# Splitting mixer steps in two, and the gate's copy ahead of the output product, in a two-layer attention and expert kernel

## The chip, the cores and the metric

The kernel runs on one core of a Trainium2 chip. The metric is the device time of one execution in microseconds (us). Three runs of the kernel before gave a median of 4238.35 us, from 4236.18 to 4253.35. A trace of one further execution (4231.16 us, of which 4229.4 lie between its first and last instruction) is what the rows below come from.

## What is computed

Two layers over 5 blocks of 128 tokens (block 0 is the prompt, blocks 1 to 4 the 512 sample tokens), all float32, width 1024. In each layer a block is normalised and modulated, multiplied by one input matrix whose columns feed three parallel mixers, and the mixed heads go through an output product that is gated and added to x. Then a product-key expert layer (PEER) follows: each token picks, for each of 8 heads, 16 of 16384 experts; every expert has one row in `u` and one in `v`.

```
x = x + g1 * (concatenate([o_na, o_pool, o_mla]) @ w_out)          # the output product and its gate
h2 = modulate(rms_norm(x, norm2), sh2, sc2)
x = x + g2 * peer(h2, wq, sub_keys, u, v)

# peer: e = the 16 best experts per head and token, g = softmax of their scores
act = gelu(einsum('nd,nhkd->nhk', xb, u[e]))
y = einsum('nhk,nhkd->nd', g * act, v[e])
```

The input product is cut into A (queries), B (keys), C (values) of the neighbourhood attention, D (pooling input and latent queries) and E (latent keys, rotary keys). A, B, D and E are RMS-normed per head or per row, and so are the up-projected latent queries ("uq") and keys ("ukv").

## The kernel before, in words

Five engines run one list of steps, the plan, each taking from it the steps in which it has work, strictly in the plan's order. The plan is built by `whole_order`.

The expert layer sets the frame. A unit is one head of one block (16 experts), so there are 80 units and 1280 rows. Step `("row", r)` means: GpSimd gathers the v rows for row r - 16 (it waits for TensorE's sum of row r - 20, whose buffer it reuses) and then the u rows for row r + 4 (it waits for VectorE's dot product of row r); VectorE forms the dot product of the u rows with the tokens and does one piece of the search for the best experts of a later unit; ScalarE writes a diagonal matrix of the expert weights; TensorE adds row r - 20 of v into `expert_sum` by two matmuls of 512 columns (the trace records four, and as many weight loads). Both rings have 4 buffers, and one gather moves 512 KB.

`weave` puts the mixer's steps between the rows: every step has a cost (`cost`, an estimate of TensorE's time), and a step is placed after the row at which half of its cost is due. The names that matter here: `pr` (projection A to E of a block), `up` and `kv` (up-projection of queries; assembly of keys), `sc` (scale a projection by its root), `us` and `ks` (the same for up-projected queries and keys, with rotation on GpSimd), `cq`, `tu`, `uT` (transposes on TensorE), `ot` (transposes of the mixed heads), `o` (one half, 512 columns, of the output product), `nx` and `nT` (second norm and its transposes), `q` (queries of the expert layer).

In a step `pr` TensorE multiplies, ScalarE squares the result, VectorE sums the squares of each head (L1432, for A and B) or copies a part (L1464, D; L1469, E), and GpSimd turns the sums into reciprocal roots, `rstd` (L980 and L983). In a step `o` TensorE first writes the gate, spread over 128 partitions, into one PSUM bank (L2052) and then the product into another (L2063). VectorE waits for both, copies the gate to `gated` (L1609), multiplies the product by it (L1611) and adds the result to x (L1614). ScalarE and VectorE count `x_updated` from the last of these. `work` in PSUM has four banks; `Banks.place` gives each result one from the step that fills it to the step that frees it (`fills_of`).

Of the kernel before, what the change touches and what calls it, by code (L numbers as in the profile page):

```python
# [7 lines left out]
D = 1024  # L8
KC = D // P
LAYERS = 2  # L10
NB = 5
# [3 lines left out]
EPS = 1e-6  # L15
HEADS = 6
# [184 lines left out]
def cost(step):  # L201
# [28 lines left out]
def heads_of_prompt(l):  # L230
    b = 0
    return [("pr", "A", l, b), ("pr", "B", l, b), ("sc", "A", l, b), ("pr", "C", l, b), ("tu", "A", l, b),
            ("sc", "B", l, b), ("pr", "D", l, b), ("tu", "B", l, b), ("sc", "D", l, b), ("pr", "E", l, b),
            ("cq", l, b), ("sc", "E", l, b), ("up", l, b), ("ck", l, b), ("us", l, b), ("kp", l, b), ("uT", l, b),
            ("kv", l, b), ("pd", l, 0, 0), ("py", l, 0, b), ("ks", l, b), ("pd", l, 0, 1), ("py", l, 1, b),
            ("kT", l, b)]


def heads_of(l, blocks):
# [6 lines left out]
    for i in range(len(products) + 2):  # L246
        slots += [[("tu", *k) for k in products[i - 2:i - 1] if i >= 2] + [("sc", *k) for k in products[i - 1:i] if i]
                  + [("pr", *k) for k in products[i:i + 1]]]
# [3 lines left out]
    for i in range(n + len(keys) + 2):  # L252
# [6 lines left out]
        out += [("pr", "D", l, b) for b in blocks[i:i + 1]]  # L259
        out += later[j:j + 1] if j >= 0 else []  # L260
        out += [("pr", "E", l, b) for b in blocks[j:j + 1] if j >= 0]
        out += [("up", l, b) for b in blocks[i - 1:i] if i]
# [6 lines left out]
        out += [("kv", l, b) for b in keys[j - 1:j] if j >= 1]  # L269
# [24 lines left out]
def tail(l, t):  # L294
# [102 lines left out]
def fills_of(step):  # L397
# [57 lines left out]
def build(nc, x_prompt, x_sample, c, c_ctx, cache_nat_k, cache_nat_v, cache_mla_ckv, cache_mla_krope,  # L455
# [6 lines left out]
    with ExitStack() as ctx:  # L462
# [172 lines left out]
        for step in plan:  # L635
            kind = step[0]
            if kind == "nx" or kind == "pr" and step[1] != "C":
                stat_turns += [step[1:]]
            elif kind in ("up", "kv"):
                stat_turns += [("uq" if kind == "up" else "ukv", *step[1:])]  # L640
            if kind == "pr" and step[1] != "C" or kind in ("up", "kv"):
                sq_turns += [stat_turns[-1]]
# [86 lines left out]
        pool_in_ready = Steps(sem("pool_in_ready"), [s[2:] if s[0] == "pr" else s[1:] for s in of_kind("pr", "pp")  # L729
                                                             if s[0] == "pp" or s[1] == "D" and not pooled_later(*s[2:])])  # L730
        rope_keys = Steps(sem("rope_keys_copied"), [s[2:] for s in of_kind("pr") if s[1] == "E"])
# [8 lines left out]
        x_updated = Steps(sem("x_updated"), of_kind("o", "fin"))  # L740
# [78 lines left out]
        def _(sp):  # L819
# [46 lines left out]
            def load_gate_bias(l, which):  # L866

                if l:
                    sp.wait_ge(*x_updated.done(("fin", NB - 1) if which else ("o", 0, NB - 1, 1)))
# [90 lines left out]
        def _(pool):  # L960
# [28 lines left out]
            def project(ch, l, b):  # L989
                if ch != "C":  # L990
                    n, mul, add = {"A": (HEADS, 1.0, DH * EPS), "B": (HEADS, 1.0 / DH, EPS),
                                   "D": (1, 1.0 / QR, EPS), "E": (1, 1.0 / KVR, EPS)}[ch]
                    rstd((ch, l, b), n, mul, add)

            def queries_up(l, b):
                rstd(("uq", l, b), HEADS, 1.0, QK * EPS)

            def keys_up(l, b):
                rstd(("ukv", l, b), HEADS, 1.0 / QK, EPS)
# [59 lines left out]
            does = {"nx": norm, "pr": project, "up": queries_up, "kv": keys_up, "us": rope_queries,  # L1059
# [7 lines left out]
        def _(sc):  # L1067
# [11 lines left out]
            def norm(k, l, b):  # L1079
# [3 lines left out]
                if k == "n2":  # L1083
                    sc.wait_ge(*x_updated.done(("o", l, b, 1)))
# [264 lines left out]
        def _(dve):  # L1349
# [107 lines left out]
            def project(ch, l, b):  # L1457

                key = (ch, l, b)
                if ch in "AB":  # L1460
# [747 lines left out]
```

## Time and profile before

| | |
|---|---|
| median of three runs | 4238.35 us |
| profiled execution | 4231.16 us |
| its span | 4229.4 us |
| mean granted TensorE clock | 0.974 |
| TensorE, matmuls | 3607.1 us (85%) |
| VectorE | 2564.7 us (61%) |
| ScalarE | 959.1 us (23%) |
| GpSimd | 2582.1 us (61%) |
| read from HBM | 1511.7 MB |

In the rows below PE is TensorE's matmuls, PEld its weight loads, DVE VectorE, ACT ScalarE, POOL GpSimd and SP SyncE; a trailing q is that engine's sequencer. L with a number is a line of the kernel. An arrow "<-" in a wait names what ended it; "issue" is time in which the engine waited for nothing that the profile shows. Rows of experts begin at 230 us.

### The profile page before, as it was taken

The page shows a single profiled execution, that of the slowest core. Times are in us where ns is not written, and L with a number is a line of the kernel's source. Part 1 is how long each engine was busy: PE and PEld are TensorE (multiplying, and loading weights), DVE is VectorE, ACT ScalarE, POOL GpSimd, SP SyncE. Part 2 cuts the span into 40 slices and gives each one's busy share as a digit, 9 for nine tenths or more (in the row PEclk, how much of TensorE's full clock was granted, in tenths as well). Part 3 has the DMA queues.
Part 4 walks back from the last instruction along what each step waited for, and adds up shares of the span by engine and source line. Part 5 has one row for each costly group of instructions (what it writes and reads, how often), then busy time and mean ns, then how long its engine had stood idle before and what let it go on. Part 6 is the DMA issues. An engine that isn't in the chain of part 4 may idle for free.

```text
span 4229.4 us, 37631 instructions
## 1 busy us (share of the span) xinstructions
PE 3607.1 (85%) x10514; PEld 1679.1 (40%) x10514; DVE 2564.7 (61%) x6453; ACT 959.1 (23%) x2479; POOL 2582.1 (61%) x2833
## 2 busy tenths in 40 slices
PE   7889899989978888888887899999898887777776
PEld 2355444545434223443342355554443432222222
DVE  1175557767655446566666555677676666666664
ACT  1212222223221112222222222232232122221211
POOL 0057446666665556676667663566676677777776
PEclk9899999999999999999999999999999999999999
DMA  6477899999999999999999988999999999999999
GB/s 241 161 266 273 296 337 388 362 389 405 358 367 379 385 390 349 344 356 360 393 401 408 353 290 297 366 367 392 392 407 351 369 402 409 407 405 405 399 403 356
DMA packets 472260, 1519.96 MB, mean 359 GB/s; under 512 B 59980, under 2 KB 78704, under 8 KB 471544
## 3 DMA queue, kind: packets, MB, share of 16 engines
q0 software_dynamic: 368640, 1342.34, 82.2%
q1 hardware_dynamic: 103416, 175.21, 11.6%
q8 instruction: 90, 1.47, 0.1%
q14 instruction: 114, 0.93, 0.1%
HBM read 1511.70 MB, written 5.67 MB: 359 GB/s over the span
## 4 chain that ended last, share of the span: by engine, by line
PE 41%; DMA 27%; POOL 15%; issue 9%; DVE 5%; ACT 2%; SPq 1%; DVEq 0%; POOLq 0%; ACTq 0%
DMA expert_rows<-in_peer_v,experts 22%; PE expert_sum L2112 21%; POOL expert_rows L1033 14%; DMA expert_rows<-in_peer_u,experts 4%; PE work L1871 4%; PE work L1845 3%; PE work L2063 3%; PE work L2078 2%; PE work L2007 2%; PE work L2034 2%; PE work L1819 2%; DVE expert_rows L1779 2%; POOL stat_rstd L983 1%; PE work L2052 1%; PE work L1963 1%
## 5 line engine op out<-in xcount | busy, mean ns | idle before, releaser
L2112 PE MATMUL expert_sum<-expert_rows,weight_diagonals 128*128 128x512 f32 x5080 | 2464.5, 615 | 450.6 <-DMA expert_rows<-in_peer_v,experts 419.8
L1779 DVE CUSTOM_DVE_ANT_0 expert_rows<-expert_rows,tokens 128x1024 f32<-128x1024 f32 x1280 | 1557.0, 1217 | 837.7 <-DMA expert_rows<-in_peer_u,experts 834.0
L1033 POOL DMA_INDIRECT expert_rows<-in_peer_v,experts x1280 | 1231.1, 962 | 915.2 <-PE expert_sum L2112 703.3
L2112 PEld LDWEIGHTS expert_sum<-expert_rows,weight_diagonals 128*128 128x128 f32 x5080 | 904.6, 193 | 1674.7 <-issue 1363.3
L1033 POOL DMA_INDIRECT expert_rows<-in_peer_u,experts x1280 | 1216.6, 950 | 452.8 <-issue 348.5
L1315 ACT ACTIVATE weight_diagonals<-ident,expert_weights 128x128 f32<-128x128 f32 x1270 | 447.2, 392 | 585.5 <-PE expert_sum L2112 355.3
L1871 PE MATMUL work<-weight_ring,h_or_mixed 128*128 128x384 f32 (+3 forms) x800 | 246.6, 462 | 4.1 <-DMA weight_ring<-in_w_in 2.3
L1819 PE MATMUL work<-ident,scratch 128*128 128x128 f32 (+1 forms) x782 | 130.6, 290 | 99.4 <-DVE scratch L1411 36.4
L1845 PE MATMUL work<-weight_ring,silu_cond 128*2 128x512 f32 x384 | 176.1, 613 | 12.0 <-DMA weight_ring<-in_w_mod 11.1
L1871 PEld LDWEIGHTS work<-weight_ring,h_or_mixed 128*128 128x128 f32 x800 | 143.9, 191 | 106.8 <-issue 49.5
L1819 PEld LDWEIGHTS work<-ident,scratch 128*128 128x128 f32 (+1 forms) x782 | 99.4, 146 | 195.3 <-issue 73.5
L1254 ACT ACTIVATE scratch<-work,neg_max 128x640 f32<-128x640 f32 (+3 forms) x120 | 77.3, 644 | 403.8 <-DVE neg_max L1570 403.6
L980 POOL TENSOR_SCALAR stat_biased<-stat_sums 128x6 f32<-128x6 f32 (+1 forms) x82 | 17.6, 214 | 242.8 <-DVE stat_sums L1432 83.8
L2078 PEld LDWEIGHTS work<-h_or_mixed,weight_ring 128*128 128x128 f32 x1024 | 143.9, 196 | 37.3 <-issue 31.4
L2078 PE MATMUL work<-h_or_mixed,weight_ring 128*128 128x128 f32 (+1 forms) x1024 | 153.7, 306 | 5.4 <-DVE h_or_mixed L1423 3.5
L2063 PE MATMUL work<-weight_ring,scratch 128*128 128x512 f32 x320 | 144.2, 604 | 0.0
L1570 DVE TENSOR_REDUCE neg_max<-work 128x1 f32<-128x640 f32 (+3 forms) x120 | 76.3, 635 | 110.7 <-PE work L2007 108.8
L1304 ACT ACTIVATE gelu_dots<-dots 128x16 f32<-128x16 f32 x80 | 17.3, 216 | 442.3 <-DVE dots L1779 441.9
L1779 DVE DVE_READ_ACCUMULATOR2_ANT dots<- 128x1 f32 x1280 | 105.0, 82 | 0.0
L1609 DVE COPY scratch<-work 128x512 f32<-128x512 f32 x20 | 13.8, 692 | 149.8 <-PE work L2063 149.8
L1304 ACT ACT_TABLE_LOAD x78 | 100.1, 1283 | 1.4
L2063 PEld LDWEIGHTS work<-weight_ring,scratch 128*128 128x128 f32 x320 | 59.8, 192 | 83.8 <-issue 83.8
(176 smaller groups left out, 2481.2 us busy)
## 6 DMA issues: line engine op xcount, KB each, us to landing
weight_ring<-in_w_mod SPq DMA_DIRECT2D x24, 2048.0 KB, 11.0
weight_ring<-in_w_out SPq DMA_DIRECT2D x16, 2048.0 KB, 19.4
weight_ring<-in_peer_wq SPq DMA_DIRECT2D x16, 2048.0 KB, 10.0
expert_rows<-in_peer_u,experts POOLq DMA_INDIRECT x1280, 7.3
expert_rows<-in_peer_v,experts POOLq DMA_INDIRECT x1280, 7.3
weight_ring<-in_w_in SPq DMA_DIRECT2D x12, 1536.0 KB, 9.5
weight_ring<-in_w_in SPq DMA_DIRECT2D x4, 2048.0 KB, 15.2
weight_ring<-in_t_pool SPq DMA_DIRECT2D x4, 2048.0 KB, 10.7
```

The lines of the kernel that those rows point to most:

```text
L1033: g.indirect_dma_start(buffer, None, table, bass.IndirectOffsetOnAxis(ap=idx_st[:, col:col + 1], axis=0),).then_inc(row_in, 16)
L1304: a_.activation(gel[:, e * TOPK:(e + 1) * TOPK], dots[:, e * TOPK:(e + 1) * TOPK], ACT.Gelu_apprx_tanh).then_inc(gelu_ready, 1)
L1315: a_.activation(diags[:, at * P:(at + 1) * P], ident[:, :], ACT.Copy, scale=wgt[:, col:col + 1]).then_inc(diag_ready, 1)
L1779: v_.tensor_tensor_reduce(out=u_ring[r % U_RING], in0=u_ring[r % U_RING], in1=tokens[:, :], scale=1.0, scalar=0.0, op0=ALU.mult, op1=ALU.a ...
L1819: ins = t_.transpose(dst[0:n, j * P:(j + 1) * P], v, ident[:, :])
L1845: ins = t_.matmul(dst[0:2, :], sct[:, :].rearrange("p (c k) -> p k c", c=2)[:, kk, :], wt[:, kk, :], start=kk == 0, stop=kk == KC - 1)
L1871: ins = t_.matmul(dst[:, lo:n], hT(b, kk), wt[:, kk, lo:n], start=kk == 0, stop=kk == KC - 1)
L2007: ins = t_.matmul(dst[:, col:col + m * P], lhs, tile(first, m)[lo:lo + n, :, pick, :], start=True, stop=True)
L2034: ins = t_.matmul(dst[:, h * DH:(h + 1) * DH], prob_T[item_no[item] % 2][:, k, :], val, start=k == 0, stop=k == len(blocks) - 1)
L2063: ins = t_.matmul(dst, o_T[:, kk, :], wt[:, kk, :], start=kk == 0, stop=kk == KC - 1)
L2078: ins = t_.matmul(dst[:, 0:len(blocks) * P], wt[:, kk, (h % 4) * P:(h % 4 + 1) * P], h_blocks[:, blocks[0]:blocks[-1] + 1, kk, :], start=k ...
L2112: ins = t_.matmul(acc[:, hf * 512:(hf + 1) * 512], diags[:, at * P:(at + 1) * P], v_buffer(row)[:, hf * 512:(hf + 1) * 512], start=first = ...
```

## The change

Two kinds of step are cut in two. `o` keeps TensorE's part, and a new step `oe` takes VectorE's part (copy, multiplication, addition); each has half of the cost, 4.4. `pr`, `up` and `kv` keep TensorE's and ScalarE's parts, and a new step `hs` of cost 0 takes VectorE's sums or copies and GpSimd's root. Since `weave` places every step by its own cost, a row can now stand between the two parts. In `oe` the wait for the product moves behind the gate's copy.

```diff
-            "kT": 1.3, "py": 0.4, "pp": 3.5, "s": 1.0, "pt": 1.0, "pv": 0.6, "ot": 1.8, "o": 8.8}.get(kind, 0.2)
+            "kT": 1.3, "py": 0.4, "pp": 3.5, "s": 1.0, "pt": 1.0, "pv": 0.6, "ot": 1.8, "o": 4.4, "oe": 4.4,
+            "hs": 0.0}.get(kind, 0.2)
...
-        out += [("pr", "D", l, b) for b in blocks[i:i + 1]]
+        out += [s for b in blocks[i:i + 1] for s in (("pr", "D", l, b), ("hs", "D", l, b))]
...
-        out += [("up", l, b) for b in blocks[i - 1:i] if i]
+        out += [s for b in blocks[i - 1:i] if i for s in (("up", l, b), ("hs", "uq", l, b))]
...
-            out += [("o", l, blocks[i], 0), ("o", l, blocks[i], 1)]
+            out += [s for j in range(2) for s in (("o", l, blocks[i], j), ("oe", l, blocks[i], j))]
...
-        return [(("g", 0, l, b, j), 1, step), (step, 1, step)]
+        return [(("g", 0, l, b, j), 1, ("oe", l, b, j)), (step, 1, ("oe", l, b, j))]
...
+            def head_roots(k, l, b):
+                n, mul, add = {"A": (HEADS, 1.0, DH * EPS), "B": (HEADS, 1.0 / DH, EPS), "D": (1, 1.0 / QR, EPS),
+                               "E": (1, 1.0 / KVR, EPS), "uq": (HEADS, 1.0, QK * EPS),
+                               "ukv": (HEADS, 1.0 / QK, EPS)}[k]
+                rstd((k, l, b), n, mul, add)
...
-            does = {"nx": norm, "pr": project, "up": queries_up, "kv": keys_up, "us": rope_queries,
+            does = {"nx": norm, "hs": head_roots, "us": rope_queries,
                     "ks": rope_keys_of, "row": expert_row}
...
                 dve.wait_ge(*banks.filled(gkey))
-                dve.wait_ge(*banks.filled(step))
                 v_.tensor_copy(gated, bank(gkey)).then_inc(banks.frees(gkey), 1)
                 dve.wait_ge(*banks.freed(gkey))
+                dve.wait_ge(*banks.filled(step))
                 v_.tensor_tensor(gated, bank(step), gated, ALU.mult).then_inc(banks.frees(step), 1)
```

What the orders become is shown at two places. The changed kernel's line numbers differ by 2 to 7. VectorE, layer 0, block 2, first half of the output product (the copy of `work` to `scratch` of 128x512, the multiplication, the addition to x) among dot products ("ISA expert_rows,dots") and pieces of the expert search; before:

```order
1010 L1779 ISA expert_rows,dots<-expert_rows,tokens 128x1024
1011 L1779 ISA dots 128x1
1012 L1676 MAX_INDEX topk<-topk 128x8
1013 L1677 TENSOR_SCALAR topk<-topk 128x1
1014 L1609 COPY scratch<-work 128x512
1015 L1611 TENSOR_TENSOR scratch<-work,scratch 128x512
1016 L1614 TENSOR_TENSOR mla_qkv_or_x_and_queries<-mla_qkv_or_x_and_queries,scratch 128x512
1017 L1779 ISA expert_rows,dots<-expert_rows,tokens 128x1024
```

and of the change, from the dot product on that now follows the same piece of the search:

```order
1015 L1773 ISA dots 128x1
1016 L1675 TENSOR_SCALAR topk<-topk 128x16
1017 L1676 TENSOR_SCALAR topk<-topk 128x16
1018 L1773 ISA expert_rows,dots<-expert_rows,tokens 128x1024
1019 L1773 ISA dots 128x1
1020 L1679 CAST topk<-topk 128x32
1021 L1773 ISA expert_rows,dots<-expert_rows,tokens 128x1024
1022 L1773 ISA dots 128x1
1023 L1683 TENSOR_TENSOR topk<-topk,iota 128x512
1024 L1602 COPY scratch<-work 128x512
1025 L1605 TENSOR_TENSOR scratch<-work,scratch 128x512
1026 L1608 TENSOR_TENSOR mla_qkv_or_x_and_queries<-mla_qkv_or_x_and_queries,scratch 128x512
```

The three instructions moved behind three further expert rows; TensorE's product moved two rows up, so that five rows lie between.

GpSimd, layer 0, from the root of projection D of block 2 (`stat_biased` and `stat_rstd` of 128x1) over that of the up-projected queries of block 1 (128x6) to their rotation (L1014 to L1021); before:

```order
81 L980 TENSOR_SCALAR stat_biased<-stat_sums 128x1
82 L983 TENSOR_TENSOR stat_rstd<-stat_biased,minus_half 128x1
83 L1033 DMA expert_rows<-in_peer_v,experts 128x1024
84 L1033 DMA expert_rows<-in_peer_u,experts 128x1024
85 L1033 DMA expert_rows<-in_peer_v,experts 128x1024
86 L1033 DMA expert_rows<-in_peer_u,experts 128x1024
87 L980 TENSOR_SCALAR stat_biased<-stat_sums 128x6
88 L983 TENSOR_TENSOR stat_rstd<-stat_biased,minus_half 128x6
89 L1033 DMA expert_rows<-in_peer_v,experts 128x1024
90 L1033 DMA expert_rows<-in_peer_u,experts 128x1024
91 L1014 TENSOR_TENSOR scratch<-scratch,bias_or_small_weights 128x6x8 x4
```

and of the change:

```order
81 L1029 DMA expert_rows<-in_peer_v,experts 128x1024
82 L1029 DMA expert_rows<-in_peer_u,experts 128x1024
83 L1029 DMA expert_rows<-in_peer_v,experts 128x1024
84 L1029 DMA expert_rows<-in_peer_u,experts 128x1024
85 L982 TENSOR_SCALAR stat_biased<-stat_sums 128x1
86 L985 TENSOR_TENSOR stat_rstd<-stat_biased,minus_half 128x1
87 L1029 DMA expert_rows<-in_peer_v,experts 128x1024
88 L1029 DMA expert_rows<-in_peer_u,experts 128x1024
89 L982 TENSOR_SCALAR stat_biased<-stat_sums 128x6
90 L985 TENSOR_TENSOR stat_rstd<-stat_biased,minus_half 128x6
91 L1010 TENSOR_TENSOR scratch<-scratch,bias_or_small_weights 128x6x8 x4
```

D's root moved behind the gathers of two rows, the queries' root behind those of one, and between the latter and the rotation no gather is left.

## Rows read from the trace of the kernel before

**Rows 1.** The page's first part, busy time, share and instructions of each engine.

```profile
PE 3607.1 (85%) x10514; PEld 1679.1 (40%) x10514; DVE 2564.7 (61%) x6453; ACT 959.1 (23%) x2479; POOL 2582.1 (61%) x2833
```

**Rows 2.** Waits of VectorE, 230 to 4229 us: us in total, times, longest.

```profile
DVE expert_rows L1779 <- DMA expert_rows<-in_peer_u,experts: 834.0, 778, 7.8
DVE scratch L1609 <- PE work L2063: 132.1, 18, 9.5
...
DVE scratch L1464 <- ACT scratch L1154: 49.3, 7, 8.3
...
DVE stat_sums L1432 <- ACT scratch L1149: 41.6, 10, 6.2
```

**Rows 3.** Waits of GpSimd, 230 to 4229 us.

```profile
POOL expert_rows L1033 <- PE expert_sum L2112: 703.3, 574, 15.7
...
POOL expert_rows L1033 <- DVE dots L1779: 85.3, 167, 3.6
```

**Rows 4.** Order of time, 876 to 900 us: start, length, instruction, [idle before].

```profile
881.00 7.13 PE L2063 MATMUL work<-weight_ring,scratch 128*128 128x512 f32 x16
...
887.97 7.03 PE L2112 MATMUL expert_sum<-expert_rows,weight_diagonals 128*128 128x512 f32 x16
...
888.27 0.69 DVE L1609 COPY scratch<-work 128x512 f32<-128x512 f32 x1 [7.36 <-PE work L2063]
...
889.72 0.69 DVE L1614 TENSOR_TENSOR mla_qkv_or_x_and_queries<-mla_qkv_or_x_and_queries,scratch 128x512 f32<-128x512 f32 x1
...
890.12 1.11 POOL L1033 DMA_INDIRECT expert_rows<-in_peer_v,experts  x1 [6.57 <-PE expert_sum L2112]
...
891.62 1.22 DVE L1779 CUSTOM_DVE_ANT_0 expert_rows<-expert_rows,tokens 128x1024 f32<-128x1024 f32 x1
891.82 0.94 POOL L1033 DMA_INDIRECT expert_rows<-in_peer_u,experts  x1 [0.59 <-DVE dots L1779]
...
895.74 0.69 DVE L1695 TENSOR_TENSOR topk<-topk 128x512 f32<-128x512 f32 x1
895.80 1.44 POOL L1033 DMA_INDIRECT expert_rows<-in_peer_v,experts  x1 [0.30 <-issue]
```

**Rows 5.** Stretches: length, busy PE, PEld, DVE, ACT, POOL, clock, DMA, GB/s.

```profile
888.00:893.00 5.00, 5.00 (x13) 2.25 (x12) 4.66 (x11) 1.78 (x3) 2.06 (x2) 1.00 0.79 273
...
283.00:454.00 171.00, 150.83 (x472) 80.55 (x473) 96.36 (x246) 44.48 (x122) 115.25 (x162) 0.98 0.80 282
...
3600.00:3700.00 100.00, 76.63 (x162) 27.27 (x160) 65.70 (x165) 19.61 (x50) 72.45 (x78) 1.00 1.02 407
```

**Rows 6.** Order of time, 1645 to 1668 us, a projection A of layer 1.

```profile
1655.12 5.31 PE L2112 MATMUL expert_sum<-expert_rows,weight_diagonals 128*128 128x512 f32 x12
...
1656.55 0.21 POOL L980 TENSOR_SCALAR stat_biased<-stat_sums 128x6 f32<-128x6 f32 x1 [1.62 <-DVE stat_sums L1432]
...
1656.84 1.36 POOL L983 TENSOR_TENSOR stat_rstd<-stat_biased,minus_half 128x6 f32<-128x6 f32 x1
...
1658.38 1.04 POOL L1033 DMA_INDIRECT expert_rows<-in_peer_v,experts  x1 [0.19 <-issue]
```

**Rows 7.** Order of time, 302 to 325 us, D and queries of layer 0.

```profile
306.90 0.57 POOL L983 TENSOR_TENSOR stat_rstd<-stat_biased,minus_half 128x1 f32<-128x1 f32 x1
...
307.95 1.01 POOL L1033 DMA_INDIRECT expert_rows<-in_peer_v,experts  x1 [0.47 <-PE expert_sum L2112]
...
313.24 1.35 POOL L983 TENSOR_TENSOR stat_rstd<-stat_biased,minus_half 128x6 f32<-128x6 f32 x1
...
314.91 0.81 DVE L1447 TENSOR_TENSOR scratch<-work,stat_rstd 128x288 f32<-128x288 f32 x2
315.05 0.44 PE L1819 MATMUL work<-ident,scratch 128*128 128x128 f32 x2 [2.01 <-DVE scratch L1491]
...
315.75 0.76 DVE L1455 TENSOR_TENSOR scratch<-scratch,gains 128x576 f32<-128x576 f32 x1
...
317.36 1.48 POOL L1014 TENSOR_TENSOR scratch<-scratch,bias_or_small_weights 128x48 f32<-128x48 f32 x4
```

More of the change, by code:

```diff
@@ L247, in heads_of @@
         slots += [[("tu", *k) for k in products[i - 2:i - 1] if i >= 2] + [("sc", *k) for k in products[i - 1:i] if i]
-                  + [("pr", *k) for k in products[i:i + 1]]]
+                  + [s for k in products[i:i + 1] for s in (("pr", *k), ("hs", *k))]]
     out = [s for slot in slots[:-2] for s in slot] + [("ct", l)] * last
@@ L268, in heads_of @@
         out += [("kT", l, b) for b in keys[j - 2:j - 1] if j >= 2]
-        out += [("kv", l, b) for b in keys[j - 1:j] if j >= 1]
+        out += [s for b in keys[j - 1:j] if j >= 1 for s in (("kv", l, b), ("hs", "ukv", l, b))]
     return out
@@ L636, in build @@
             kind = step[0]
-            if kind == "nx" or kind == "pr" and step[1] != "C":
+            if kind in ("nx", "hs"):
                 stat_turns += [step[1:]]
+            if kind == "pr" and step[1] != "C":
+                sq_turns += [step[1:]]
             elif kind in ("up", "kv"):
-                stat_turns += [("uq" if kind == "up" else "ukv", *step[1:])]
-            if kind == "pr" and step[1] != "C" or kind in ("up", "kv"):
-                sq_turns += [stat_turns[-1]]
+                sq_turns += [("uq" if kind == "up" else "ukv", *step[1:])]
             if kind == "sc":
@@ L728, in build @@
         rope_step = sem("rope_step")
-        pool_in_ready = Steps(sem("pool_in_ready"), [s[2:] if s[0] == "pr" else s[1:] for s in of_kind("pr", "pp")
+        pool_in_ready = Steps(sem("pool_in_ready"), [s[2:] if s[0] == "hs" else s[1:] for s in of_kind("hs", "pp")
                                                              if s[0] == "pp" or s[1] == "D" and not pooled_later(*s[2:])])
-        rope_keys = Steps(sem("rope_keys_copied"), [s[2:] for s in of_kind("pr") if s[1] == "E"])
+        rope_keys = Steps(sem("rope_keys_copied"), [s[2:] for s in of_kind("hs") if s[1] == "E"])
         values_ready = Steps(sem("mla_values_ready"), [s[1:] for s in of_kind("kp")])
@@ L868, in load_gate_bias @@
                 if l:
-                    sp.wait_ge(*x_updated.done(("fin", NB - 1) if which else ("o", 0, NB - 1, 1)))
+                    sp.wait_ge(*x_updated.done(("fin", NB - 1) if which else ("oe", 0, NB - 1, 1)))
                 at = (3 * which + 2) * D
@@ L1083, in norm @@
                 if k == "n2":
-                    sc.wait_ge(*x_updated.done(("o", l, b, 1)))
+                    sc.wait_ge(*x_updated.done(("oe", l, b, 1)))
                     if b == 0:
@@ L1455, in gain_mul, with sums_of_heads @@
                 v_.tensor_tensor(view, view, g, ALU.mult).then_inc(gained.sem, 1)
-            def project(ch, l, b):
-                key = (ch, l, b)
-                if ch in "AB":
+            def sums_of_heads(k, l, b):
+                key = (k, l, b)
+                if k in ("A", "B"):
                     head_sums(key, heads(sq[:, 0:WIDTH]))
-                elif ch == "D" and not pooled_later(l, b):
+                elif k in ("uq", "ukv"):
+                    head_sums(key, heads(sq))
+                elif k == "D" and not pooled_later(l, b):
                     dve.wait_ge(*stats.filled(key))
                     v_.tensor_copy(pool_in[:, max(b - 1, 0), :], bank(key)[:, 0:POOL_W]).then_inc(pool_in_ready.sem, 1)
-                elif ch == "E":
+                elif k == "E":
                     dve.wait_ge(*stats.filled(key))
@@ L1793, in expert_row @@
                     v_.tensor_tensor(block_sum[:, :], acc[:, :], block_sum[:, :], ALU.add).then_inc(sum_copied, 1)
-            does = {"vec": vectors, "mcol": mod_cols, "mrow": gate_row, "nx": norm, "nT": norm_evac, "pr": project, "pp": pool_part, "sc": scale,
-                    "up": queries_up, "us": scale_queries, "kv": assemble, "ks": scale_keys, "py": pooled,
-                    "s": score_maxima, "pt": turn_probs, "pv": head_values, "o": mixer_out, "top": first_topk,
+            does = {"vec": vectors, "mcol": mod_cols, "mrow": gate_row, "nx": norm, "nT": norm_evac, "hs": sums_of_heads, "pp": pool_part, "sc": scale,
+                    "us": scale_queries, "kv": assemble, "ks": scale_keys, "py": pooled,
+                    "s": score_maxima, "pt": turn_probs, "pv": head_values, "oe": mixer_out, "top": first_topk,
                     "fin": finish, "row": expert_row}
```

33 lines of the change are left out of this document (11 added, 22 removed).

## The prediction

> **What bounds the kernel now.** I read the page's busy shares first and then stretches of 100 us and more. TensorE is busy 3607.1 of 4229.4 us, VectorE and GpSimd 61% each [rows 1]. In a stretch that holds expert rows and nothing else the DMA share is 1.02 and the rate 407 GB/s; in the stretch of layer 0's projections, from 283 to 454 us, it is 0.80 and 282 GB/s, with TensorE busy 150.83 of 171 us [rows 5]. So the expert rows, one u and one v row of 512 KB each at a time, want the whole DMA; time is lost only where something keeps GpSimd from issuing the next gather, or where TensorE has so much mixer work that the sums are the pace. The waits of GpSimd say which of the two: between 230 us and the end it waited 703.3 us, 574 times, for an expert sum of TensorE, and 85.3 us, 167 times, for a dot product of VectorE [rows 3].
>
> VectorE's own waits name the steps of this change. It waited 132.1 us, 18 times, for the output product (L2063, in front of the copy L1609); 49.3 us in front of the copy of the pooled part (L1464) and 41.6 us in front of the head sums (L1432), both for ACT squares that stand behind a projection [rows 2]. That is 223 us of a waiting VectorE, but it waited 834.0 us for u rows as well: it has time to spare. Whether these stalls cost anything is decided by what stands behind them, so I then read two products in order of time.
>
> **One output product, read instruction by instruction** [rows 4]. The 16 matmuls of the product take 7.13 us from 881.00. TensorE then sums four rows in 7.03 us from 887.97, so the first sum is there at about 889.7. VectorE starts its copy at 888.27, 7.36 us after it fell idle, adds to x from 889.72, and is free at 890.4. GpSimd had nothing to issue for 6.57 us: the v gather at 890.12 waited for the sum, not for VectorE. Its next gather, of a u row at 891.82, waited 0.59 us for a dot. After that a dot takes VectorE 1.22 us, and GpSimd needs 1.24 us for each gather (0.94 and 0.30 between two) and two gathers per row, so VectorE catches up faster than GpSimd asks. In these 5 us the DMA moved 273 GB/s instead of 407 [rows 5], a loss of 5 x (1 - 273/407) = 1.65 us. The cause of that hole is that TensorE is blocked for 7 us and the v gather in GpSimd's queue stands in front of the u gather. The change leaves both as they are; it takes away only the part that VectorE adds.
>
> **The change part by part.** All sums are against the profiled execution, 4231.16 us (span 4229.4); the median of the runs shown, 4238.35, is 7.2 us above it.
>
> 1. The gate's copy without the wait for the product. Only in three of the 20 places do the two steps stand with no expert row between: both halves of layer 0's prompt, and the first half of its block 1. In the prompt the copy, 0.69 us [rows 4], leaves the chain behind the second product; behind the first the second product hid it in any case. In block 1 it shortens the stall by as much. Sum: -1 us. In the other 17 the copy does not run during the product at all: it now stands 1 to 5 expert rows behind it.
>
> 2. Those 17 steps, VectorE's side. The stall of about 7.3 us goes, since the product is long done when oe comes up. What GpSimd gains is the excess of its waits for dots: 0.59 us where a plain hand-over is 0.30, once or twice per product. 17 x 0.3 = -5 us. From above this is bounded by 0; from below by all excess of the 167 waits, 85.3 - 167 x 0.30 = 35 us [rows 3]. I take -5, since the timeline shows the single event.
>
> 3. The roots (rstd) of projections A and B. Before, GpSimd meets them before the next row's gathers: it waits 1.62 us for the head sums, then works 0.21 + 1.36 us, and its next v gather starts at 1658.38 [rows 6]. Without them the gather could follow the first of the three sums that start at 1655.12 and take 5.31 us, so at about 1657.0: 1.4 us earlier. Nine A and B keys that are followed by sums move so, -13 us. The same 1.57 us come back one to three rows later; where GpSimd waits for a sum then, they are hidden, where it does not, they cost +14. With 703.3 us over 574 waits GpSimd mostly has slack, in these stretches less. Bounds -13 and +1; I take the middle, -6.
>
> 4. The roots of D and E, 15 moved. Before, they lie in a wait: 0.57 us from 306.90, and the v gather at 307.95 then waits another 0.47 us for the sum [rows 7]. Behind a row's gathers they are 0.78 us (0.21 [rows 6] + 0.57) of GpSimd work in the open. Bounds 0 and 15 x 0.78 = +12; I take +3, since GpSimd is idle soon after in most cases.
>
> 5. Scaling of the up-projected queries. In five places (layer 0, blocks 1, 2 and 4; layer 1, blocks 0 and 4) the order now has root, scale and rotation with no expert row between. Before, two gathers lie between the root (from 313.24) and the rotation (317.36), and VectorE's scale and gain (0.81 and 0.76 us) run beside them [rows 7]. Now GpSimd has to wait for them: 0.81 + 0.76 + hand-overs, 1.9 us. Bounds 0 and 5 x 1.9 = +9. Behind the wait stand the gathers of the next row, and VectorE in turn waits for the root (1.35 us) with that row's dot behind it. At 317 us TensorE goes into a 7 us projection, during which GpSimd is idle anyway, so +3.
>
> 6. The scale of D. Its transposes on TensorE waited 2.01 us at 315.05 because VectorE came late, with a row's dot product between head sums and scale [rows 7]. VectorE now has rows done while the projection runs, but its root arrives later. I put it at half, nine D keys x 0.5 = -4; bounds 0 and nine x 2.0 us, of which 9 is the most I believe, since the other waits in this place are shorter.
>
> 7. The addition to x meets other work. A gather that ran beside a VectorE instruction with two SBUF inputs (the 128x512 product of the index search at 895.74) took 1.44 us instead of 0.94 [rows 4]. The addition L1614 has two such inputs. Before it ran where GpSimd had just been released and stretched a gather to 1.11; now it runs in the middle of rows. Bounds 0 and 17 x (0.50 - 0.17) = +6; I take +2.
>
> Here the Trainium skill (SBUF - State Buffer, section Who interferes with whom) speaks against the change: a VectorE instruction with two SBUF inputs contends with a GpSimd instruction that reads SBUF, and the loser is blocked for the whole instruction. The stretched gather agrees. Taken at full length, the page would have each of the 17 additions of 0.69 us hold a gather up by that much, about 12 us as an estimate by that page, where the trace shows 0.50.
>
> TensorE's order: the output products stand up to 3 expert rows earlier than before, each as long as it was. The gate's and the product's banks are held some rows longer. Both at nothing: two of the four banks are left, and the experts' scores need one per 16 rows. If a transpose or a score had to wait for them, each such wait would be a few rows of 2.6 us (1.05 MB at 407 GB/s), and that is in the range, not in the sum.
>
> Sum: -1 - 5 - 6 + 3 + 3 - 4 + 2 = -8, so 4223 us by the profiled execution and 4230 by the median.
>
> **The rivals.**
>
> *The stalls were on the path after all (a real gain).* For it: the chain that ended last does run from the product through copy, product, addition and dots into the gathers; VectorE's stalls add up to 223 us. If each of the 17 holes closed by its 1.65 us, that is -28 in place of the -5, so -31 in all: 4207. With every bound at its lower end (-35, -13, -9, -1) it is -58: 4180. Against it: at 890.12 the gather was released by the sum, and that sum is not earlier.
>
> *GpSimd pays for it (slower).* Roots that lay in waits now stand between gathers. If GpSimd has no slack in the two stretches with projections, items 3, 4, 5 and 7 stand at their upper ends: 1 + 12 + 9 + 6 = +28 with nothing gained: 4266. For it: at 1.24 us per gather two of them take 2.5 us of the 2.6 us that a row takes at full DMA rate, and behind a product GpSimd issues back to back. Against it: TensorE is 88% busy there [rows 5], and GpSimd then waits for it. It decides if GpSimd's waits for sums fall to nearly nothing between 283 and 454 us.
>
> *It doesn't do what it says.* The copy overlaps a product in 3 of 20 places, and if VectorE's stalls were covered in full, the roots in full too, the time stays at 4238.
>
> **How the numbers follow.** My forecast has 0.50, the real gain 0.24, GpSimd pays 0.16, nothing at all 0.10. About 0.5% (21 us, so 4217 and 4260) is what a measurement of this kernel can tell from no change. The gain counts as faster, with 0.02 from the forecast's own low edge: 0.26. Slower is 0.16, and the rest, 0.48 + 0.10 = 0.58, lies within. The range takes in most of each rival: 4190 to 4262. The forecast's own range is 4217 to 4245.
>
> **What would show it.** Right: 17 of the 18 waits in front of the gate's copy gone, and GpSimd's wait for sums behind each output product still 6 to 7 us; the waits for stat_sums in front of the roots near zero, with the lost time under expert_sum in their place; DMA about 273 to 300 GB/s in the 5 us behind a product, as before; a new GpSimd wait of 1 to 2 us in front of the rotation in five places. Wrong: rows between 230 and 631 us, or 1600 and 1900, that advance clearly faster or slower than before, or the hole behind a product gone.

## The result, and the profile after

The changed kernel takes 4265.41 us, median of five runs (4254.86 to 4268.83), against 4238.35 for the kernel before (five runs, 4232.10 to 4253.35). The ratio is 1.0061, 95% interval 1.0046 to 1.0075: the medians are 27 us apart, and the time lies outside the range of 4190 to 4262. The profiled execution took 4256.04 us, its span 4254.2, so 24.8 us more than the span before. The page's first part answers to [rows 1]:

```profile
PE 3625.7 (85%) x10514; PEld 1686.6 (40%) x10514; DVE 2566.1 (60%) x6453; ACT 960.9 (23%) x2479; POOL 2578.0 (61%) x2833
```

No engine has more instructions, and VectorE and GpSimd have the same work to within about 4 us. The time is in waits, and in TensorE's matmuls, as many as before and busy 18.6 us longer (see the granted clock below). VectorE's, from the first expert rows to the end (us in total, times, longest), answer to [rows 2]:

```profile
DVE expert_rows L1773 <- DMA expert_rows<-in_peer_u,experts: 941.0, 819, 8.2
DVE scratch L1443 <- POOL stat_rstd L985: 108.3, 32, 6.4
...
DVE scratch L1489 <- POOL stat_rstd L985: 33.6, 10, 6.6
...
DVE scratch L1462 <- ACT scratch L1150: 19.4, 5, 7.5
...
DVE scratch L1605 <- PE work L2057: 15.6, 4, 6.3
```

The waits that the change was to remove are mostly gone: 132.1 us in front of the copy became 15.6 in front of the multiplication, 49.3 in front of D's copy 19.4. Two other waits took their place. L1443 (head scale, L1447 before) and L1489 (scale of D and E, L1491 before) wait for GpSimd's root. The prediction names this wait in one clause of item 5, for the up-projected queries, and touches it in item 6 for D. In the kernel before, the same two rows read:

```profile
DVE scratch L1447 <- POOL stat_rstd L983: 42.7, 15, 6.1
...
DVE scratch L1491 <- POOL stat_rstd L983: 5.4, 3, 2.1
```

So 48.1 us in 18 waits became 141.9 in 42. GpSimd's waits answer to [rows 3]:

```profile
POOL expert_rows L1029 <- PE expert_sum L2106: 774.4, 614, 14.6
...
POOL scratch L1010 <- DVE scratch L1451: 19.3, 11, 1.8
```

GpSimd waits more for sums, not less: it did not become the bound. It also waits more for dot products, 96.0 us against 85.3. Its waits for head sums (L982) are nearly gone, 8.7 us, as foreseen.

**Where the time is lost.** Every row has one dot product of VectorE, so the time from one dot to a later one compares both kernels stretch by stretch (us, profiled executions; "other chip" is one on which the kernel before takes 4414 us):

| rows | before | after | the change again, other chip | what stands there |
|---|---|---|---|---|
| start to row 0 | 229.8 | 225.4 | 225.7 | prompt |
| 0 to 20 | 52.7 | 61.4 | 61.5 | A and B, layer 0 |
| 20 to 60 | 170.9 | 179.8 | 180.5 | A to E, queries and keys |
| 60 to 400 | 1115.6 | 1115.1 | - | with the output products of layer 0 |
| 400 to 480 | 262.5 | 264.9 | 265.2 | projections of layer 1 |
| 680 to 700 | 86.0 | 96.6 | 95.5 | D and E, layer 1, block 3 |
| 760 to 1279 | 1419.4 | 1416.0 | - | output products, then rows alone |

Three stretches of 80 rows in all lose 8.7 + 8.9 + 10.6 = 28.2 us, and the prompt, 4.4 us shorter for another reason (below), gives 24.8 together with small differences elsewhere. Rows 60 to 400, with the output products of layer 0, neither won nor lost.

**Rows 0 to 20, the first place.** Layer 0, order of time (start, length, instruction, [idle before]); first before, where the dot of 234.45 lies between the head sums and the scale:

```profile
233.99 0.55 DVE L1432 TENSOR_REDUCE stat_sums<-scratch 128x6 f32<-128x384 f32 x1
234.45 1.21 DVE L1779 CUSTOM_DVE_ANT_0 expert_rows<-expert_rows,tokens 128x1024 f32<-128x1024 f32 x1
...
236.56 0.56 DVE L1447 TENSOR_TENSOR scratch<-work,stat_rstd 128x384 f32<-128x384 f32 x1
```

then after, where nothing lies between:

```profile
231.71 0.55 DVE L1428 TENSOR_REDUCE stat_sums<-scratch 128x6 f32<-128x384 f32 x1
...
232.65 1.37 POOL L985 TENSOR_TENSOR stat_rstd<-stat_biased,minus_half 128x6 f32<-128x6 f32 x1
234.16 0.56 DVE L1443 TENSOR_TENSOR scratch<-work,stat_rstd 128x384 f32<-128x384 f32 x1 [1.89 <-POOL stat_rstd L985]
...
236.73 1.05 POOL L1029 DMA_INDIRECT expert_rows<-in_peer_u,experts  x1 [2.71 <-DVE dots L1773]
```

GpSimd needs 1.37 us for the root in either kernel, and 0.20 for a scaling ahead of it [rows 6]. Before, VectorE did a dot and a piece of the search meanwhile; now it stands for 1.89 us, the dot behind it is late, and the next gather, which waits for that dot, is 2.71 us idle. There is no expert sum in these rows, and VectorE waits for hardly anything but roots: VectorE is the pace. Its waits for roots in this stretch, before and after:

```profile
DVE scratch L1447 <- POOL stat_rstd L983: 3.4, 2, 2.0
```

```profile
DVE scratch L1443 <- POOL stat_rstd L985: 11.8, 6, 2.7
```

That is 8.4 us more of waiting in a stretch that is 8.7 us longer.

**Rows 680 to 700, the dearest place.** Projection D of layer 1, block 3, before:

```profile
2451.82 0.42 DVE L1464 COPY scratch<-work 128x256 f32<-128x256 f32 x1 [6.66 <-ACT scratch L1154]
2451.88 0.19 POOL L980 TENSOR_SCALAR stat_biased<-stat_sums 128x1 f32<-128x1 f32 x1 [3.00 <-ACT scratch L1154]
...
2455.16 0.47 DVE L1491 TENSOR_SCALAR scratch<-work,stat_rstd 128x256 f32<-128x256 f32 x1
...
2455.68 0.77 PE L1819 MATMUL work<-ident,scratch 128*128 128x128 f32 x5 [1.06 <-DVE scratch L1491]
```

and after:

```profile
2466.61 0.42 DVE L1462 COPY scratch<-work 128x256 f32<-128x256 f32 x1 [1.89 <-ACT scratch L1150]
...
2467.97 0.94 POOL L1029 DMA_INDIRECT expert_rows<-in_peer_v,experts  x1 [3.81 <-PE expert_sum L2106]
...
2472.99 0.57 POOL L985 TENSOR_TENSOR stat_rstd<-stat_biased,minus_half 128x1 f32<-128x1 f32 x1
2473.67 0.48 DVE L1489 TENSOR_SCALAR scratch<-work,stat_rstd 128x256 f32<-128x256 f32 x1 [6.63 <-POOL stat_rstd L985]
...
2474.20 1.33 PE L1813 MATMUL work<-ident,scratch 128*128 128x128 f32 x5 [4.79 <-DVE scratch L1489]
...
2479.11 1.01 POOL L1029 DMA_INDIRECT expert_rows<-in_peer_v,experts  x1 [5.56 <-PE expert_sum L2106]
```

The long wait in front of D's copy has shrunk from 6.66 to 1.89 us. But the root now stands in GpSimd's queue behind the gathers of two rows, the first of which waits for the sum behind the projection. The root is made 6.4 us after the copy (2472.99 against 2466.61) instead of 0.3. VectorE waits 6.63 us with no row in between, TensorE waits 4.79 us for VectorE with its sums queued behind the transposes, and GpSimd waits for those sums: a circle through three engines. The chain that ended last in this window runs right along it, from the gathers over the root (2472.99) to (start, length, what):

```profile
2473.67 0.49 DVE scratch L1489
...
2474.20 1.33 PE work L1813 x5
2475.53 3.30 PE expert_sum L2106 x4
```

**The granted clock.** In two of the three stretches TensorE also works longer for the same matmuls. Rows 680 to 700 before and after, then rows 20 to 60 after, which answer to the second line of [rows 5] (stretch, length, busy PE, PEld, DVE, ACT, POOL, clock, DMA share, GB/s):

```profile
2441.00:2527.00 86.00, 79.91 (x262) 44.87 (x262) 47.55 (x121) 22.57 (x63) 55.65 (x80) 1.00 0.80 285
```

```profile
2455.00:2552.00 97.00, 84.55 (x266) 47.23 (x265) 48.10 (x122) 23.00 (x63) 56.23 (x81) 0.93 0.74 256
```

```profile
287.00:467.00 180.00, 156.71 (x474) 83.18 (x474) 96.76 (x246) 44.73 (x122) 116.21 (x163) 0.94 0.75 268
```

From 2470 to 2475 us TensorE, waiting for the scale, was busy 0.80 of 5 us; the granted clock was 0.68 in these 5 us and 0.64 in the next five, so in part at the lower of its two levels (1.2 of 2.4 GHz), and 1.00 again from 2480. In the kernel before it was 1.00 in all of rows 680 to 700. Read from the busy times, this makes TensorE about 4 us longer in rows 680 to 700 and about 6 in rows 20 to 60. As an estimate, that is 4 of the 10.6 us and 6 of the 8.9: part of what a root's wait costs is paid behind it, in slower matmuls. No run separates the two. In rows 0 to 20 the clock falls as well (1.00 to 0.92), but VectorE, the pace there, waits for nothing of TensorE's.

**Why the order lost its row.** `hs` has cost 0. `weave` places a step after the row at which half of its cost is due; for a step without cost that is the very end of its product's share. The step that uses the root (`sc`, `us`, `ks`) has cost 0.2, half of which is due at nearly the same point. Before, sums and root stood with the product, at the middle of its share, and one to three rows came before the scale. In 16 places none is left. Call them the uncovered keys: in layer 0 projections A of blocks 1, 2 and 4, B of 2, D of 1, E of 3, the queries of 1, 2 and 4; in layer 1 A of 0 and 4, B and D of 3, E of 4, the queries of 0 and 4. Twelve of them lie in the three stretches that lose time (four, five and three). The other four stand at rows 421, 469, 676 and 678; rows 400 to 480 lose 2.3 us, and rows 480 to 680 nothing (609.5 us before, 608.9 after).

### The profile page after: what moved, and what is told of

Its sections match the earlier page's. It is cut to its first block, busy times and chain, and to the rows that moved or that the text cites. A ratio compares the mean times of both kernels' runs of the same rounds, so it can differ in the third digit from the quotient of the medians.

```text
span 4254.2 us, 37644 instructions
## 1 busy us (share of the span) xinstructions
PE 3625.7 (85%) x10514; PEld 1686.6 (40%) x10514; DVE 2566.1 (60%) x6453; ACT 960.9 (23%) x2479; POOL 2578.0 (61%) x2833
## 4 chain that ended last, share of the span: by engine, by line
PE 41%; DMA 28%; POOL 16%; issue 10%; DVE 4%; ACT 1%; SPq 1%; POOLq 0%; DVEq 0%; ACTq 0%
DMA expert_rows<-in_peer_v,experts 24%; PE expert_sum L2106 23%; POOL expert_rows L1029 14%; PE work L1839 4%; DMA expert_rows<-in_peer_u,experts 3%; PE work L1865 3%; PE work L2057 3%; PE work L2072 2%; PE work L2001 2%; PE work L2028 2%; PE work L1813 2%; POOL stat_rstd L985 1%; DVE expert_rows L1773 1%; PE work L1957 1%; PE work L2046 1%
## 5 line engine op out<-in xcount | busy, mean ns | idle before, releaser
L982 POOL TENSOR_SCALAR stat_biased<-stat_sums 128x6 f32<-128x6 f32 (+1 forms) x82 | 17.6, 214 | 194.8 <-ACT expert_rows L1106 70.9
L1839 PEld LDWEIGHTS work<-weight_ring,silu_cond 128*2 128x2 f32 x384 | 31.3, 86 | 143.8 <-issue 142.1
## 6 DMA issues: line engine op xcount, KB each, us to landing
weight_ring<-in_w_mod SPq DMA_DIRECT2D x24, 2048.0 KB, 10.6
```

The lines of the kernel that those rows point to most:

```text
L1839: ins = t_.matmul(dst[0:2, :], sct[:, :].rearrange("p (c k) -> p k c", c=2)[:, kk, :], wt[:, kk, :], start=kk == 0, stop=kk == KC - 1)
```

## The experiments

All ran on other chips, where the kernel before takes 4413.97 and 4414.92 us (medians of 32 and of 31 runs), so ratios count: 0.1% is 4.4 us there. The times expected for numbers 1 to 4 are those of the first chip, to be read against its 4238 us. Three explanations were on record. COVER: VectorE waits for the roots of the 16 keys because no row covers GpSimd's work. QUEUE: what costs is the root's later place in GpSimd's queue, between gathers. PRODUCT: the halves `oe` cost, by their new place or by the additions beside gathers. In these kernels helper functions stand ahead of `whole_order`, and line numbers are 34 to 41 higher. `rejoin(plan, pick)` puts the picked `hs` or `oe` steps back directly behind their product.

**1. Only the output product split.**

```diff
-    return plan
+    return rejoin(plan, lambda s: s[0] == "hs")
```

> Only the output product is split (o and oe as in the change); every hs stands directly behind its product, as before the change. Theory COVER (the loss is that VectorE now meets 16 scalings with no expert row between the sums and the scaling, and waits for GpSimd's root): none of it is here, 4232 to 4240. Theory QUEUE (31 roots now stand between gathers on GpSimd): the same, 4232 to 4240. Theory PRODUCT (the later addition to x, or the banks held longer, is the loss): 4258 to 4268.

Measured 4411.15 us, ratio 0.9991 (0.9977 to 1.0005). Rows 0 to 20 take 53.4 us, rows 680 to 700 85.7. Its waits:

```profile
DVE scratch L1477 <- POOL stat_rstd L1019: 43.5, 16, 5.8
...
DVE scratch L1639 <- PE work L2091: 16.3, 4, 6.3
```

The product's stall is gone as in the changed kernel, the waits for roots are as before, and the time is the time before. PRODUCT falls. Some 116 us of VectorE's waiting were removed for at most a quarter of a per cent.

**2. Only the sums split**, the output product whole again and at its old place:

```diff
-"o": 4.4, "oe": 4.4,
+"o": 8.8, "oe": 0.0,
...
-    return plan
+    return rejoin(plan, lambda s: s[0] == "oe")
```

> Only the sums and roots are split off (hs as in the change); copy, multiplication and addition stand directly behind the output product, as before, with the copy ahead of the wait. COVER and QUEUE: the whole loss is here, 4260 to 4270. PRODUCT: 4235 to 4245.

Measured 4431.86 us, ratio 1.0040 (1.0023 to 1.0056). The product's stall is there again and still the loss is the change's (1.0048, 1.0033 to 1.0064, for the changed kernel on the same kind of chip, number 5):

```profile
DVE scratch L1477 <- POOL stat_rstd L1019: 107.2, 32, 6.4
DVE scratch L1639 <- PE work L2091: 99.9, 18, 6.7
...
DVE scratch L1523 <- POOL stat_rstd L1019: 32.8, 9, 6.6
```

**3. The row kept.** The change, but the sums of the 16 uncovered keys put back with their products:

```diff
-    return plan
+    return rejoin(plan, lambda s: s[0] == "hs" and uncovered(plan, s))
```

> The change, but the 16 hs steps behind which the use of the root (sc or us) comes with no expert row between, and which had a row before, go back directly behind their product; the other 15 or so stay moved. COVER: the loss goes, the 5 us gained in rows 408 to 460 stay, 4228 to 4240; VectorE's waits for roots fall from 142 us (108.3 + 33.6) to about 60. QUEUE: half of the roots still stand between gathers, 4248 to 4256. PRODUCT: 4260 to 4268.

Measured 4413.56 us, ratio 0.9998 (0.9984 to 1.0012). 16 of the steps `hs` carry the whole loss. VectorE's waits for roots (the two groups above) fell to 78.6 us, not to the expected 60 or so.

**4. The scale later.** The change, its sums and roots where the change has them, but the 16 scalings moved behind the next expert row, so that a row covers the root again:

```diff
+    for step in [s for s in plan if s[0] == "hs" and uncovered(plan, s)]:
+        use = use_of(step)
+        i = plan.index(use)
+        j = next(n for n in range(i, len(plan)) if plan[n][0] == "row")
+        plan = plan[:i] + plan[i + 1:j + 1] + [use] + plan[j + 1:]
```

> The change, but in those 16 places it is the use of the root (sc or us) that moves: behind the next expert row, so that one row lies between the late sums and the scaling again. All roots stand between gathers as in the change. COVER: 4232 to 4246, a little above row_kept, since TensorE's transposes may wait for the later scaling. QUEUE: 4262 to 4270, nothing is mended. PRODUCT: 4262 to 4270.

Measured 4409.57 us, ratio 0.9995 (0.9981 to 1.0010). Number 3 could not tell COVER from QUEUE, since it moves the roots back as well; here they stay late in GpSimd's queue and the loss is gone all the same. But 680 to 700 takes 92.9 us in this kernel's profile, against 87.2 in number 3: there one row does not cover a root that is made 6 us late. In that place the root's later turn between gathers, the term of QUEUE, does count, but by making the wait long.

**5. The changed kernel again**, as the mark for numbers 6 to 8.

> The changed kernel itself, beside the kernel before on this chip, as the measure for the three others: 1.004 to 1.008 times before.

Measured 4436.97 us, ratio 1.0048 (1.0033 to 1.0064). The stretches given in the table above repeat on this chip within 1.1 us.

**6. No wait for the root.** The order of the change on every engine, and GpSimd makes every root in its place, but the 16 scalings multiply by a constant column instead of the root (so their result is another) and need not wait:

```diff
-                r = stat_cols(rst, key, 8)[:, h0:h0 + n]
+                r = (half if key in UNCOVERED else stat_cols(rst, key, 8))[:, h0:h0 + n]
...
-                dve.wait_ge(*rstd_ready.done(key))
+                if key not in UNCOVERED:
+                    dve.wait_ge(*rstd_ready.done(key))
```

> The change with the same instructions in the same order on every engine, but the 16 uncovered scalings take a constant column in place of the root and don't wait for it (their projections come out scaled wrongly); GpSimd makes every root where the change has it. COVER: the loss is this wait, so 0.996 to 1.002 times before. QUEUE (the roots' place between GpSimd's gathers): as the change, 1.004 to 1.008.

Measured 4410.60 us, ratio 0.9994 (0.9980 to 1.0009). At the first place the scale follows the sums at once and the root is made for nobody:

```profile
232.45 0.55 DVE L1466 TENSOR_REDUCE stat_sums<-scratch 128x6 f32<-128x384 f32 x1
232.92 0.55 DVE L1481 TENSOR_TENSOR scratch<-work,minus_half 128x384 f32<-128x384 f32 x1
...
233.38 1.37 POOL L1023 TENSOR_TENSOR stat_rstd<-stat_biased,minus_half 128x6 f32<-128x6 f32 x1
```

Rows 0 to 20 take 53.1 us and rows 680 to 700 85.5, as before. The order of GpSimd's queue is the change's, and by itself it costs nothing that can be measured. QUEUE falls as a cost of its own; this is the run that shows COVER. The granted clock in rows 680 to 700 is 1.00 again, so the slower matmuls go with the wait. From 1.0048 to 0.9994 are 24 us for 16 waits, 1.5 us each on average.

**7. Only the uncovered sums moved**, the other `hs` back with their products:

```diff
-    return plan
+    return rejoin(plan, lambda s: s[0] == "hs" and not uncovered(plan, s))
```

> The opposite of row_kept: of the hs steps only the 16 uncovered ones stand where the change has them, all others go back directly behind their product; the output product is split. COVER: the whole loss, 1.004 to 1.009 times before. QUEUE: half of it, 1.002 to 1.004.

Measured 4440.52 us, ratio 1.0056 (1.0035 to 1.0077): the full loss from the 16 alone, the mirror of number 3. VectorE's waits for roots sum to 106.2 us here, with the whole loss, and to 111.3 us in number 4, with none. So their sum does not tell the cost; in number 4 the wait stands behind the row's dot product instead of in front of it.

**8. More cover than before.** If a covering row is worth 1.5 us, then giving one to places that never had one should make the kernel faster than before. Number 1, with the keys' scalings (`ks`) of eight places that stand right behind their sums moved behind the next row:

```diff
+    plan = rejoin(plan, lambda s: s[0] == "hs")
+    for step in [s for s in plan if s[0] == "hs" and s[1] == "ukv" and rows_between(plan, s, use_of(s)) == 0]:
+        use = use_of(step)
+        i = plan.index(use)
+        rows = [n for n in range(i, len(plan)) if plan[n][0] == "row"]
+        if rows and rows[0] < plan.index(("kT", *use[1:])):
+            plan = plan[:i] + plan[i + 1:rows[0] + 1] + [use] + plan[rows[0] + 1:]
```

> x_only (only the output product is split), and in eight places where the kernel before has sums and scaling of the up-projected keys with no expert row between, the scaling (ks) moves behind the next row. COVER predicts a gain of 8 x about 2 us, 16 us, where TensorE, VectorE and GpSimd set the pace (six of the eight), so 0.996 to 0.998 times before and below both kernels. QUEUE: nothing, 0.998 to 1.001.

Measured 4412.68 us, ratio 1.0003 (0.9987 to 1.0019): a miss, and in the range that was expected of QUEUE. The waits did go:

```profile
DVE scratch L1484 <- POOL stat_rstd L1026: 23.7, 14, 3.8
```

against 43.5 in number 1, and 20 us fewer of waiting bought nothing that can be measured. In the same two profiles VectorE's waits in front of the head sums rose from 84.6 to 99.7 us, so in part it only waited elsewhere. In single profiles rows 20 to 60 take 168.6 us against 171.2 and rows 680 to 700 84.6 against 85.7, but rows 60 to 100 181.2 against 180.0. So 1.5 us is no price of a wait as such. The 16 cost what they do because of where they stand: where VectorE is the pace (rows 0 to 20) or where TensorE has its sums queued behind the scaled result (2474.20 above). This is read from two places in order of time; rows 20 to 60 were not read so, and no run moves single ones of the 16. None of these kernels is measurably faster than the kernel before; the lowest ratio is 0.9991.

## Why the prediction was wrong

The forecast was a sum of -8 us; the change cost 27. By its items:

- **Items 1, 2 and 7, the output product** (-1, -5 and +2, together -4): not contradicted. Number 1 is this part alone, 0.9991 of 4238 or -4 us, but with an interval of -10 to +2, which takes in nothing at all, so the agreement to the microsecond is luck. The reason held. The v gather behind a product still waits for the sum and the DMA's hole is unchanged, against 6.57 us in [rows 4] and 273 GB/s in [rows 5] (the second fence: stretch of 5 us, busy PE, PEld, DVE, ACT, POOL, clock, DMA share, GB/s):

```profile
898.28 0.95 POOL L1029 DMA_INDIRECT expert_rows<-in_peer_v,experts  x1 [6.39 <-PE expert_sum L2106]
899.53 0.94 POOL L1029 DMA_INDIRECT expert_rows<-in_peer_u,experts  x1 [0.30 <-issue]
```

```profile
896.00:901.00 5.00, 5.00 (x13) 2.24 (x12) 2.68 (x7) 0.80 (x2) 2.11 (x3) 1.00 0.80 263
```

  The 0.59 us in front of the u gather became 0.30, just the bit that item 2 counted. Item 7's +2 was not there: 7 of the 20 additions held a gather up in the profile after, by 0.09 to 0.48 us and 2.0 us in all, against 17 and 2.9 us before. The sign that it named came only in part: 14 of the 18 waits went, not 17. Four remain, now in front of the multiplication.
- **Items 3 and 4, the roots** (-6 and +3): the wrong engine was priced. They ask only what GpSimd gains or loses when a root moves behind gathers, and number 6, which keeps those moves, comes out at 0.9994 (0.9980 to 1.0009), so at nothing that can be measured. Who waits for the root was not asked there, although the root has one reader, the scale, on an engine that works in order.
- **Item 5 is the step that failed.** It says "in five places ... the order now has root, scale and rotation with no expert row between", and takes +3. It looked for a row between root and rotation, on GpSimd, for the queries alone. It does add that "VectorE in turn waits for the root (1.35 us) with that row's dot behind it", which is the mechanism, but only for these five places, and it was set off against a projection of TensorE. The row that mattered lies between VectorE's own sums and VectorE's own scale. It is gone in 16 places, 11 of them of A, B, D and E, where the term stood at nothing except for D's later root in item 6. Together they cost 24 us; rows 0 to 20, which hold four of A and B and no queries, lose 8.7. The wait it did describe is real and as long as it said (1.8 us), but there are three more of them instead of five, 19.3 us in all against 12.7.
- **Item 6, the scale of D** (-4): wrong in sign. That "its root arrives later" was seen and valued at less than the rows gained. TensorE's waits for the scales of D and E sum to 17.2 us before, the longest 2.3, and to 22.8 after, the longest 4.8.

- **Rows 0 to 20 were in no item by their place.** The prediction began with "time is lost only where something keeps GpSimd from issuing the next gather, or where TensorE has so much mixer work that the sums are the pace". The first half of that is true there, since the gathers wait for late dots (25.2 us against 15.2 before), but the count of what delays a dot was missing. In the first 20 rows VectorE is the pace: it is busy 47.58 of 53 us before and 48.21 of 62 after, the same work (columns as above, VectorE's share is the third):

```profile
230.00:283.00 53.00, 42.99 (x145) 24.45 (x143) 47.58 (x125) 10.87 (x26) 33.27 (x38) 1.00 0.81 273
```

```profile
225.00:287.00 62.00, 48.21 (x146) 26.39 (x145) 48.21 (x128) 10.96 (x26) 32.99 (x37) 0.92 0.71 237
```

  A reading by stretch would have shown it, and one key there with its 1.57 us root and no row between gives the 1.9 us seen.
- **The rivals.** The slower one gave 4266, nearly the time measured, by a mechanism that is not there. It was to decide by GpSimd's waits for sums falling to nearly nothing in layer 0's projections. They rose from 12.9 us in 8 waits to

```profile
POOL expert_rows L1029 <- PE expert_sum L2106: 26.3, 9, 6.4
```

  and number 6 leaves GpSimd's work and order as they are and loses nothing. That its 4266 lies beside 4265.41 is luck. The real gain did not come, since the hole behind a product is TensorE's. The sign of being wrong that the prediction named did come: rows between 230 and 631 us before, rows 0 to 100, took 400.7 us and now take 419.8.

What stays open: rows 400 to 460 gain 5.0 us in the changed kernel and rows 460 to 480 give 7.4 back. Numbers 3, 4 and 6 show the same pair (194.9 to 196.5, then 67.0 to 67.7), and numbers 1, 7 and 8 do not (201.9 to 204.4, then 60.8 to 62.6), so it goes with the `hs` steps that are not among the 16. It sums to little and was not followed. The changed kernel's granted clock is also a little lower as a whole (median 0.961 in its 12 runs of number 5, 0.963 in the 31 of the kernel before beside them). Among these 31 runs 0.001 less goes with 1.9 us more, so that is about 4 of the 22 us as an estimate, and it is not shown which is cause and which effect.

## What to carry to other kernels

When an order written out for several in-order engines is changed, follow each moved result to its reader and count what that reader has left to do between asking and getting; a step of cost nothing in a planner is placed hard against the next one, and takes away the work that covered its latency. A long wait of an engine with slack (132 us here) can be free and a new one of 1.9 us dear: price a wait by the stretch it stands in, by who is the pace there and by what stands behind it in the waiting engine's order, and read the first rows and the odd stretches apart from the average. A rival whose number fits is not thereby shown; the run that keeps its mechanism and removes the other's decides.

## What the runs showed of the hardware

**A VectorE instruction with two SBUF inputs that begins before a gather holds it up, and the gather then ends 0.82 us after it.** Item 7 put the stretch at 0.50 us. In the changed kernel, order of time, three places:

```profile
671.32 1.57 POOL L1029 DMA_INDIRECT expert_rows<-in_peer_u,experts  x1 [0.30 <-issue]
...
671.38 0.68 DVE L1683 TENSOR_TENSOR topk<-topk,iota 128x512 f32<-128x512 f32 x1
...
908.32 0.69 DVE L1683 TENSOR_TENSOR topk<-topk,iota 128x512 f32<-128x512 f32 x1
908.39 1.44 POOL L1029 DMA_INDIRECT expert_rows<-in_peer_v,experts  x1 [0.40 <-PE expert_sum L2106]
...
910.13 0.95 POOL L1029 DMA_INDIRECT expert_rows<-in_peer_u,experts  x1 [0.30 <-issue]
...
910.37 0.69 DVE L1608 TENSOR_TENSOR mla_qkv_or_x_and_queries<-mla_qkv_or_x_and_queries,scratch 128x512 f32<-128x512 f32 x1
```

The second gather ends at 909.83, 0.82 us after the index search. All 14 gathers between 630 and 1000 us that a product of the search or the addition to x stretched (0.99 to 1.57 us long) end 0.81 to 0.83 us after that instruction. The third gather was 0.24 us old when the addition began, and took 0.95 like any other. The whole trace gives the rule. In 64 cases such an instruction of 128x512 began at least 0.05 us before the gather and had at least 0.13 us left to run; these gathers took 0.95 to 1.44 us, and 63 of them end 0.81 to 0.83 us after it (one 0.92). In 58 cases it began later than that, up to 0.25 us into the gather; 57 of these gathers took 0.95 us at most. The exception is the first one shown, 1.57 us long, whose instruction is recorded 0.06 us behind it; it stays unexplained. So the one that begins first goes first, and a meeting costs a gather between nothing and 0.50 us by chance of place. The prediction cited the Trainium skill (SBUF - State Buffer, section Who interferes with whom) and said that the trace shows less than its full blocking. Read by ends instead of lengths, the trace agrees with the page: the order of issue decides who blocks, and a gather is held up to the end of the instruction.

**The clock in the prompt.** The granted clock between 180 and 185 us was 0.64 before, so in part at the lower level, and 1.00 after; in these 5 us TensorE did 8 and 13 groups of instructions (columns as above):

```profile
180.00:185.00 5.00, 5.00 (x8) 2.08 (x8) 0.00 (x0) 0.00 (x0) 0.00 (x0) 0.64 0.01 3
```

```profile
180.00:185.00 5.00, 5.00 (x13) 2.28 (x12) 0.00 (x0) 0.00 (x0) 0.00 (x0) 1.00 0.00 0
```

The first expert row comes 4.4 us earlier in the kernel after. It is not the change's doing in any way that was found: numbers 1 and 8 have the same instructions in the same order on every engine up to the first rows, and reach row 0 at 229.8 us (clock 0.61 in these 5 us) and 225.2 us (1.00). What decides it was not tried.

**Chips differ in what the expert rows get.** From 3600 to 3700 us, rows alone, the kernel before moved 407 GB/s on the first chip [rows 5] and the changed kernel 406. Number 1, on another chip:

```profile
3600.00:3700.00 100.00, 72.53 (x156) 26.76 (x157) 61.08 (x159) 20.11 (x47) 66.93 (x71) 0.98 0.98 369
```

That is 9% less, and rows 760 to 1279 take 1524.8 us there against 1419.4 in the kernel before on the first chip: 105 of the 176 us between 4238 and 4414. The loss of the change is about the same on both, 27 us (0.46 to 0.75%) and 22 (0.33 to 0.64%); it arises in stretches where the DMA is not full (share 0.71 to 0.75 after).
